# Block products for six groups of the first feed-forward input projection, and the output weight of the second mixer split in four pieces

## What is computed

```python
def swiglu_ffn(h, w_ffn_in, w_ffn_out):
    gate, up = jnp.split(h @ w_ffn_in, 2, axis=-1)
    return (jax.nn.silu(gate) * up) @ w_ffn_out
...
    o = lax.map(block, (qn_b, qp_b, jnp.arange(N)))        # latent attention of the second block, 8 heads
...
    x = x + jnp.einsum('bsm,md->bsd', mixed, w_out[l])     # mixed: retention beside latent attention
```

## Time and profile before

| | |
|---|---|
| median of 3 runs | 1401.46 us (1401.24 to 1401.70) |
| the profiled execution | 1401.97 us, its span 1400.2 us |
| TensorE | busy 96% of the span, mean granted clock 0.991 |
| VectorE, ScalarE, GpSimd | busy 70%, 49%, 8% |
| `ffn_in0` | from 392.6 to 483.1 us |
| `ffn_out0`, `ffn_in1` | from 483.1 and from 527.1 us |
| latent attention, values of heads 0 to 7 | from 938 to 982.4 us |

### The profile page before, as it was taken

How to read it: one execution, slowest core, us unless ns; L and a number is a source line. 1 busy time by engine, 2 the same in 40 slices (tenths; PEclk the granted TensorE clock), 3 DMA queues, 4 the chain that set the end, 5 groups by cost and what they waited for, 6 DMA issues and landing times. The chain is left out here.

```text
span 1400.2 us, 18267 instructions
## 1 busy us (share of the span) xinstructions
PE 1347.5 (96%) x7031; PEld 1142.9 (82%) x7031; DVE 975.5 (70%) x1195; ACT 689.6 (49%) x919; POOL 108.7 (8%) x73
## 2 busy tenths in 40 slices
PE   7999999999889999999999999988999999999997
PEld 5789888877568889988999887778878888888885
DVE  4899988778854499846848758887557745663663
ACT  4333777674454245533545855668355423441442
POOL 0000000011100096000012000000110000000001
PEclk9999999999999999999999999999999999999998
DMA  9444211147543423232252251210223232222221
GB/s 378 184 165 119 77 60 45 30 151 269 196 151 135 142 91 113 99 121 90 84 188 68 69 158 46 68 46 31 81 78 113 90 108 87 106 90 94 88 81 68
DMA packets 27892, 156.09 MB, mean 111 GB/s; under 512 B 3312, under 2 KB 3824, under 8 KB 14640
## 3 DMA queue, kind: packets, MB, share of 16 engines
q1 hardware_dynamic: 27824, 155.17, 31.9%
HBM read 145.98 MB, written 4.19 MB: 107 GB/s over the span
## 5 line engine op out<-in xcount | busy, mean ns | idle before, releaser
L1749 DVE TENSOR_TENSOR w_lo<-raw,w_hi 128x2048 fp32r<-128x2048 f32 (+2 forms) x128 | 253.1, 1977 | 82.2 <-ACT w_hi L1072 68.3
L1072 ACT ACTIVATE w_hi<-raw 128x2048 fp32r<-128x2048 f32 (+2 forms) x89 | 159.9, 1797 | 102.7 <-PE psum L604 62.7
L604 PE MATMUL psum<-h_hi,w_hi 128*128 128x512 f32 x440 | 112.0, 393 | 2.3 <-DVE w_lo L1749 2.1
L604 PE MATMUL psum<-h_hi,w_lo 128*128 128x512 f32 x440 | 110.9, 391 | 0.0
L604 PE MATMUL psum<-h_lo,w_hi 128*128 128x512 f32 x440 | 110.1, 389 | 0.0
L604 PEld LDWEIGHTS psum<-h_hi,w_hi 128*128 128x128 f32 x440 | 81.0, 188 | 20.3 <-DVE w_lo L1749 4.0
L604 PEld LDWEIGHTS psum<-h_lo,w_hi 128*128 128x128 f32 x440 | 82.6, 188 | 17.2
L604 PEld LDWEIGHTS psum<-h_hi,w_lo 128*128 128x128 f32 x440 | 82.0, 188 | 17.0
L604 PE MATMUL psum<-xg_hi,w_hi 128*128 128x512 f32 x336 | 83.0, 389 | 0.0
L604 PE MATMUL psum<-xg_lo,w_hi 128*128 128x512 f32 x336 | 83.0, 389 | 0.0
L604 PE MATMUL psum<-xg_hi,w_lo 128*128 128x512 f32 x336 | 83.0, 389 | 0.0
(11 more groups left out here) (427 smaller groups left out, 2933.1 us busy)
## 6 DMA issues: line engine op xcount, KB each, us to landing
raw<-w_ffn_in SPq DMA_DIRECT2D x22, 1024.0 KB, 4.8
raw<-w_up SPq DMA_DIRECT2D x22, 1024.0 KB, 4.8
ada_first<-ada SPq DMA_DIRECT2D x16, 512.0 KB, 11.0
raw<-w_gate SPq DMA_DIRECT2D x8, 1024.0 KB, 4.9
raw<-w_mix_out SPq DMA_DIRECT2D x8, 1024.0 KB, 4.9
raw<-w_ffn_out SPq DMA_DIRECT2D x8, 1024.0 KB, 4.8
raw<-w_down SPq DMA_DIRECT2D x8, 1024.0 KB, 4.8
ada_mid<-ada SPq DMA_DIRECT2D x11, 512.0 KB, 5.4
```

What stands on the lines that cost most here:

```text
L604: last = mm(ps, w[slot][:, k, t * P:(t + 1) * P], part(xv, k0 + k), start=first, stop=final)
L1072: A(w_hi[slot][:, 0:stage.kc, :], raw[slot][:, 0:stage.kc, :], ACT.Copy).then_inc(sem["w_hi_done"], 1)
L1749: return tt(out_lo, full, high.bitcast(F32), ALU.subtract)
```

## The change

It does three things.

1. Groups 2 to 7 of `ffn_in0` are folded (`FOLDS` gives the first folded group of each stage); groups 0 and 1 stay plain. The sums of the input are made on VectorE after the weight split of group 1, ahead of taking out group 0. t4's split is put into the folded loop (`late_high`, `late_low`). The blocks of the input and the weight are now the even and the odd chunks. The column of `ada_last` of a folded group comes at the end of the next group's turn. In its new place t3 and t4 have buffers of their own; `ada_last` now lies where y is, so ScalarE waits for all columns before it writes y.
2. GpSimd starts the angles when `ffn_in0` is done on TensorE, and waits for the columns before the second half of them. The positions are loaded earlier.
3. The split of the first group of `mix_out2` is divided in four: ScalarE copies two chunks in each turn of heads 3 to 6, VectorE subtracts two in each turn of heads 4 to 7.

```diff
-FOLDS = ["ffn_in1", "ffn_in2"]
+FOLDS = {"ffn_in0": 2, "ffn_in1": 0, "ffn_in2": 0}
...
# TensorE, folded
                     elif p == 7:
-                        pe.wait_ge(sem["fold_lo"], FOLD_T["lo"] + 2 * nth + 2)
+                        pe.wait_ge(sem["fold_lo"], 2 * nth + 2)
+                        pe.wait_ge(sem["t_lo_done"], parts_done - 1)
...
                     elif p == 3:
                         pe.wait_ge(sem["w_lo_done"], stage.g0 + g + 1)
-                        pe.wait_ge(sem["fold_out"], 2 * nth + 1)
+                        pe.wait_ge(sem["fold_out"], read_count[name, g, 5])
+                    elif p == 4:
+                        pe.wait_ge(sem["t_lo_done"], parts_done)
...
-                else:
-                    gemm(st["ffn_in0"], h_hi, h_lo, ready=("made_lo", MADE["pre_ffn"], 0))
+                if r == 0:
+                    gemm(st["ffn_in0"], h_hi, h_lo, ready=("made_lo", MADE["pre_ffn"], 0), steps=(0, 1))
+                    gemm(st["ffn_in0"], h_hi, h_lo, steps=(1, FOLDS["ffn_in0"] // 2))
+                folded(st[f"ffn_in{r}"], *h_parts, T_PARTS)
...
# ScalarE
+            for k in range(FOLDS["ffn_in0"]):
+                def ahead():
+                    if k + 1 < FOLDS["ffn_in0"]:
+                        split_hi(first, k + 1, (k + 1) % 2, (k + 1) // 2)
+                    else:
+                        for _ in fold_highs(first, k + 1):
+                            pass
+                gated(first)(k // 2, k % 2, k, ahead)
+                if k == 0:
+                    fold_input_highs()
...
             def first_out(i, s, k, ahead):
 
+                if k == 0:
+                    act.wait_ge(sem["ada_sum"], 6 * DC)
                 to_y(st["ffn_out0"])(i, s, k, ahead)
-                if k == 1:
-                    fold_input_highs()
...
-                if n == PAIRS:
-                    split_hi(st["mix_out2"], 0, 0, 0)
+                if n >= PAIRS - 1 and n < HEADS - 1:
+                    mix_high(n - PAIRS + 1)
...
# VectorE
+            for k in range(FOLDS["ffn_in0"]):
+                def ahead():
+                    if k + 1 < FOLDS["ffn_in0"]:
+                        split_lo(first, k + 1, (k + 1) % 2)
+                    else:
+                        fold_split(first, k + 1)
+                    if k == 0:
+                        fold_input_sums()
+                    elif k == 1:
+                        fold_input_lows()
+                gated(first, 0)(k // 2, k % 2, k, ahead)
...
                     if not final:
                         fold_sums(stage, g + 1)
                         fold_lows(stage, g + 1)
-                    if g:
+                    if g == begin and late_low:
+                        late_low()
+                    if g > begin:
                         first_half(g - 1)
                         gate(g - 1)
...
-                if n == PAIRS:
-                    split_lo(st["mix_out2"], 0, 0)
+                if n >= PAIRS:
+                    mix_low(n - PAIRS)
...
# GpSimd
             pool.wait_ge(sem["in_rows"], 48)
-            pool.wait_ge(sem["ada_sum"], 6 * DC)
+            pool.wait_ge(sem["tile_done"], 2 * st["ffn_out0"].g0)
             step(nc.gpsimd.tensor_copy(pos_f[:, :], pos_i[:, :]))
             for kind, sin_t, cos_t in (("ret", sin_ret, cos_ret), ("mla", sin_mla, cos_mla)):
+                if kind == "mla":
+                    pool.wait_ge(sem["ada_sum"], 6 * DC)
```

More of the change, by code:

```diff
@@ L157, in up_release, with fold_order @@
     return ("uk_lo", 2 * (j + 1 - UP_K)) if j < UP_V else ("uv_lo", j + 1 - UP_V)
-def fold_order(n):
+def fold_order(begin, n):
     out = []
-    for g in range(n):
+    for g in range(begin, n):
         out += [(g, 1), (g, 7)]
@@ L171, in fold_order @@
     return out
-FOLD_SIGNALS = (1, 7, 6, 2, 5, 3)
 def fold_counts(st):
[L179 to L192, removed]
+    mm, seed, read, nth = {}, {}, {}, {}
+    for name, begin in FOLDS.items():
+        for g, p in fold_order(begin, st[name].n):
+            if p != 4:
+                mm[name, g, p] = len(mm) + 1
+        for g in range(begin, st[name].n):
+            nth[name, g] = len(nth)
+            for p in (1, 6) if name.startswith("down") else (1, 7, 6, 0):
+                seed[name, g, p] = len(seed) + 1
+            for p in (0, 5) if name.startswith("down") else (5, 4):
+                read[name, g, p] = len(read) + 1
+    return mm, seed, read, nth
+T_SUMS, T_PARTS = 8, 4
+PAIR_SUMS, DOWN_SUMS, DOWN_PARTS = 3, 15, 5
 def positive(v):
@@ L1110, in ahead @@
                             split_hi(stage, 2 * i + s + 1, 1 - s, i + s)
-                        elif stage.next and stage.next.name in FOLDS:
+                        elif stage.next and FOLDS.get(stage.next.name) == 0:
                             for _ in fold_highs(stage.next, 0):
@@ L1396, in product_high @@
                     A(mid_hi[:, g, :], act_p[g % 2][:, :], ACT.Copy).then_inc(sem["mid_hi_done"], 1)
-                for g in range(stage.n):
+                for g in range(begin, stage.n):
                     final = g == stage.n - 1
@@ L1805, in ahead @@
                             split_lo(stage, 2 * i + s + 1, 1 - s)
-                        elif stage.next and stage.next.name in FOLDS:
-                            fold_sums(stage.next, 0)
-                            fold_lows(stage.next, 0)
-                            fold_last(stage.next, 0)
+                        elif stage.next and FOLDS.get(stage.next.name) == 0:
+                            fold_split(stage.next, 0)
                         elif stage.next:
@@ L2196, in first_out @@
-            def first_out(i, s, k, ahead):
-                ahead()
-                if k == 0:
-                    fold_input_sums()
-                elif k == 1:
-                    fold_input_lows()
+                for n, (hi, lo, full) in enumerate(((t3_hi, t3_lo, t3_f[1][:, :, :]), (t1_hi, t1_lo, t1_f[:, 1]), (t2_hi, t2_lo, t2_f[:, 1]))):
+                    dve.wait_ge(sem["t_hi_done"], n + 1)
+                    if n == 0:
+                        dve.wait_ge(sem["t_sum"], T_SUMS)
+                    less(lo, full, hi).then_inc(sem["t_lo_done"], 1)
@@ L2537, in mla_out_low, with mix_low @@
                 less(h_lo[:, 2 * i, :], o_raw[i][:, :], h_hi[:, 2 * i, :]).then_inc(sem["mos_lo"], 1)
+            def mix_low(piece):
+                two = slice(2 * piece, 2 * piece + 2)
+                if piece == 3:
+                    dve.wait_ge(sem["w_hi_done"], st["mix_out2"].g0 + 1)
+                last = less(w_lo[0][:, two, :], raw[0][:, two, :], w_hi[0][:, two, :])
+                if piece == 3:
+                    last.then_inc(sem["w_lo_done"], 1)
             mla_max(0)
```

284 lines of the change are left out of this document (154 added, 130 removed).

## The result

The changed kernel takes 1404.97 us (median of 15 runs, 1403.67 to 1408.14), the kernel before 1401.61 beside it (15 runs, 1400.54 to 1404.91). The medians are 3.4 us apart. The ratio, worked out from all runs, is 1.0020, with an interval of 1.0012 to 1.0028: slower by 2.8 us, between 1.7 and 3.9. The profiled execution has a span of 1402.3 us, 2.1 above that of before (1400.2).

A forecast was written before the change was run, and what follows sets the result against it. TensorE, busy 96% of the span, was taken as the bound, with its waits deciding each stage. Stage +7.7 (12.6 - 4.9), GpSimd -0.6, split -1.6 gave +5.5 us: median 1407.0, range 1402.5 to 1411.5.

The forecast's parts named there:

- the two small pieces: Gains outside the first input projection: -0.6 us beside GpSimd and -1.6 us from splitting the `mix_out2` weight in four.
- 10.08 us a folded group: TensorE in `ffn_in0`: six folded groups take 60.5 us in place of 65.4, -4.9 us if nothing makes it wait.
- (2,3) later than TensorE could start it: In `ffn_in0`, VectorE's in-order work delays this block product to 440.4 where 427.8 was due: +12.6 us.
- beside GpSimd: Input sums leave GpSimd's stretch and the angles start earlier, so a 0.93 us stop may vanish: -0.6 us, bounds -0.9 and +0.5.
- the split in four: Heads: 3.03 us back, 0.5 lost to pieces, new 0.9 stop before the last projection: -1.6 us, bounds -3.0 and +0.5.
- VectorE's chain: In `ffn_in0`, VectorE's ordered work from 406.73 (sums, taking out, weight splits, low parts) ends at 440.4 with the addition for (2,3).
- rival 2: All small terms fall well, with cheaper 256-column matmuls: no difference, +0.8 us, 1402.3; chance 0.11.
- Ahead of VectorE throughout: In `ffn_in0`, ScalarE's copies for the input low parts take 1.05 us each, start at 417 and never hold VectorE up.
- The clock: Low clock after the two new `ffn_in0` stops costs 1.7 us, hidden in 2.7 us left; if not hidden, stage +11.0.
- rival 3: The low clock isn't hidden in the stage and falls before the output projection too: 1412.4 us; chance 0.12.
- Loads: Group, column and position loads on SyncE's queue cost nothing; the stage's last column has bounds 0 to +0.5 us.
- Rival 1: VectorE's sums fit its idle time beside the first group, so the kernel gets faster, 1394.1 us; chance 0.09.

The follow-up runs named there:

- Experiment 3: Changed kernel with three more 128x1024 additions on VectorE ahead of the input sums: 1408.17 us, stage 101.06 us against 97.66.
- experiment 2: Kernel before with only ScalarE's loop over the eight groups of `ffn_in0` written out as straight instructions: 1400.51 us, ratio to before 0.9993.
- experiment 5: Changed kernel with GpSimd's angles waiting for the last modulation column, as in the kernel before: 1404.48 us, ratio to before 1.0020.
- experiment 8: Changed kernel folded from group 4 on, input sums spread over VectorE's gaps, both queues in order of need: 1394.32 us, ratio to before 0.9941.
- 10, first kernel: Changed kernel with only groups 6 and 7 folded, sums spread, seed and (g,3) addition moved earlier: 1395.38 us, ratio to before 0.9957.
- experiment 7: Changed kernel folded from group 4 on, four sums each behind groups 0 and 1, queues not otherwise reordered: 1403.40 us, ratio to before 1.0008.
- experiment 6: Changed kernel with eight additional, unused 128x1024 additions on VectorE beside `ffn_out0`: 1413.23 us, ratio to before 1.0085.

## Why the prediction was right, and where not

The forecast was +5.5 us and 1407.0, with a loss in the stage given back in part by the two small pieces. The measured change is +3.4 in the medians (+2.8 by the ratio of all runs) and +2.1 in the profiled executions, within the range and slower as forecast. It lies on the border of the 2.8 us that the prediction asked of "slower". The mechanism is as it was argued; four terms have another size. That the stage came out so near (+7.1 for +7.7) is in part luck: two errors, of -1.5 and +1.1, worked against each other. The two small pieces gave back 4.7 us, where 2.2 were forecast.

| term | forecast | measured |
|---|---|---|
| 10.08 us a folded group | -4.9 | -4.8 (1.44 us a product over 35) |
| (2,3) later than TensorE could start it | +12.6 | +13.5 |
| group 1 earlier | not seen | -1.5 |
| beside GpSimd | -0.6 | -2.1 |
| the split in four | -1.6 | -2.6 |

- **TensorE's own work**: right. The spacing of 1.44 us a product held from 439.82 to 490.22, so a product has no cheaper form in this stage than in the next. The shorter isolated gap of the Trainium skill's page "TensorE: Matmul & The Clock Gate" ("Back-to-back issue gap") would make the 35 products 45.9 us, an estimate from the page; the trace, with 50.40 us, doesn't agree.
- **VectorE's chain**: right in its steps, the sums 9.20 us for the 9.2 forecast, (2,1) at 421.46 for 422.9, (2,7) at 427.76 for 429.1, (2,3) at 439.82 for 440.4. The first two are earlier by 1.4 and 1.3 us, nearly the 1.5 of group 1; the last by 0.6. Experiment 3 shows that the chain sets them all, (2,3) by way of ScalarE's seed. One sum of the prediction was wrong: twelve operations at 1.1 us in place of 1.14 end 0.5 us earlier and not 0.8, so the lower bound of the stage was +7.2 (and rival 2 1402.6).
- **The step that failed first** is the start of that chain. I took "from 406.73, when the weight of group 1 is split" from the earlier trace rows as given. The change writes ScalarE's first groups out, and with the loop goes a table load of 1.28 us. I read the diff for what it moves on each engine and not for what a loop had cost. 1.5 us; experiment 2.
- **ScalarE was given no term.** "Ahead of VectorE throughout" held for the copies of the three input sums (415.71 to 418.65), and I counted nothing else for it. But its seed of (2,6), a copy that must stand in PSUM before (2,5), stood behind the high part of group 3's sums, which waits for VectorE, and behind the late high part: a stop of 1.62 us ahead of (2,5). I had costed ScalarE by its busy time and not by its order. The stop delays (2,3) by 1.1 us, which hides that the chain ended 1.7 us earlier than forecast (438.74 for 440.4).
- **The clock**: hidden, as taken, though with little room. Matmuls took nearly twice as long behind both stops (0.85 us for four, 0.48 later), to 431.2. From (2,7) at 427.76 six products are 8.6 us and the low clock adds some 1.7, to 438.1; VectorE had the chain to finish until 438.7. So rival 3 falls, by some 0.7 us. Nor did the new stop ahead of `mix_out2` lower the clock.
- **GpSimd**, forecast -0.6 with bounds -0.9 and +0.5, was out of its bounds. I counted the one stop of the earlier trace rows and nothing else in `ffn_in1`; the stage as a whole gave 1.67 us and `ffn_out0` 0.43. And I put it down to the earlier start, which is 0.47 of it (experiment 5).
- **The split in four**: -2.6 for -1.6. The 0.5 us that I counted for the pieces wasn't there: turns with a piece are 5.67 us apart. And I had counted only one turn as disturbed. Before, the low clock reached into the next one: from 971.77 to the transposes of head 7 in the row below it took 6.21 us, now 5.67. The new stop was 0.82 for the 0.9 forecast. The last piece begins 0.6 us after the operation ahead of it, as forecast.

```profile
977.98 1.31 PE L1016 MATMUL psum<-ident,mp 128*128 128x128 f32 x10
```

- **Loads**: nothing lost, as taken. The last column waited 1.22 us for its load, and the split behind it still came in time.

Rival 1, sums hidden, was the right question asked of the wrong place. The idle time of VectorE in the earlier trace rows is real: started two groups later and put in the gaps, the same sums and the fold's start cost the stage 2 us (experiment 8: 87.9 for 90.55 - 1.43 - 4 x 0.80 = 85.9) or 0.4 us (10, first kernel: 87.9 for 87.5), and these kernels are 10 us faster than the changed one.

## What to carry to other kernels

When a preparation is to be hidden beside a stage, write the queue of the engine that does it as a list with due times, from the first instruction to the last one that another engine waits for, and do the same for every engine that waits for it: starting the new form two groups later gave up 1.6 us of savings, and together with the order of both queues it gave back 10. Starting later alone (experiment 7) shortened the stage by 2.2 us, with the order by 9.7. A saving per group is small (0.8 us here), so one stop eats several groups. An additional operation costs its full time or nothing, by where it stands, and the same holds for a wait put ahead of work that is due.

## What the runs showed of the hardware

- Behind the stops of 4.87 and 3.37 us in the changed kernel the granted clock was 0.50 (until 431.2), behind the one of 1.62 us ahead of (2,5) it stayed at 1.00. For how long it stays low isn't a matter of the stop alone: behind stops of 1.84 and 1.83 us, with the same work behind them, 3.4 and 6.8 us. Behind the stop of 3.99 us ahead of `ffn_in0`, the first group took 12.83 to 13.75 us in kernels that had nothing different there. That is 1.4 and 0.9 us of difference between executions that no edit explains.
- Beside GpSimd, VectorE's addition of 128x1024 took 1.75 us and not 1.14. GpSimd's own 31 operations took 51.4, 52.8 and 62.1 us beside a VectorE busy 29.8, 36.8 and 57.6 us. The Trainium skill ("SBUF — State Buffer", "SBUF: two separate sides") says that the two take a shared pair of memory ports in turn, each for a whole instruction, where VectorE reads two operands from SBUF and GpSimd reads SBUF too; the additions and subtractions of the splits do. The trace agrees in direction for VectorE's addition and for the two ends of GpSimd's times; that eight such additions stretched GpSimd by only 1.4 us (experiment 6) it doesn't explain.
- Inside a loop ScalarE loaded a function table ahead of a copy, 1.28 us, which the same copy in straight instructions didn't need (experiment 2).
